# The last down-projection groups by output chunk, the next norm's sums under them, and the second block's output projection as three fp32r products

## The reference: what is computed

```
# first block
h = concatenate([meta, x])
for l in range(2):
    hn = rmsnorm(h, norm1_g[l])
    ...
    h = h + concatenate([attn_out, conv_out]) @ w_out[l]
    hn = rmsnorm(h, norm2_g[l])
    gate, up = split(hn @ w_gate_up[l])
    h = h + (silu(gate) * up) @ w_down[l]        # 2816 -> 1024
h = rmsnorm(h, final_g)                          # the second block's x
# second block
h = rms(x, g_mix) * (1 + sc1) + sh1
proj = h @ w_in
...
merged = sigmoid(gate_a) * (y_a @ w_up_gdn) + sigmoid(gate_b) * (y_b @ w_up_dil)
x = x + gt1 * (merged @ w_out)                   # 1024 -> 1024
h2 = rms(x, g_ffn) * (1 + sc2) + sh2
x = x + gt2 * moe_ffn(h2)
```

## Time and profile before

| what | value |
|---|---|
| median of 3 runs | 1787.42 us (1782.62, 1787.43, 1787.42) |
| the profiled execution's own time | 1784.96 us |
| its span, first to last instruction | 1783.1 us |
| TensorE matmuls busy | 1709.4 us (96%) |
| DVE busy | 910.5 us (51%) |
| ACT busy | 682.7 us (38%) |
| mean granted TensorE clock | 0.983 of 2.4 GHz |
| HBM read | 401.39 MB |

### The profile page before, as it was taken

The page is one execution under the profiler, slowest core; times in us unless marked ns, Lnnn a source line. Parts: engine busy times, 40 slices in busy tenths (PEclk is TensorE's granted clock), DMA queues, the critical chain, the costliest instruction groups (busy, mean ns, idle before and its releaser), DMA issues.

```text
span 1783.1 us, 28470 instructions
## 1 busy us (share of the span) xinstructions
PE 1709.4 (96%) x11058; PEld 1335.9 (75%) x11058; DVE 910.5 (51%) x1612; ACT 682.7 (38%) x1242; POOL 55.8 (3%) x48
## 2 busy tenths in 40 slices
PE   7998999989989999999999999899999999999997
PEld 5777999987779999977889899898545454545453
DVE  4957666438757665367765778844211212121212
ACT  2136444321264443254654377722122222222222
POOL 0001000000010000003220000000000000000000
PEclk9999999999999999998999999998999999999999
DMA  6534454545434555532422344355699999999993
GB/s 272 199 142 144 164 175 179 189 142 195 183 142 146 186 188 189 189 116 95 138 70 78 112 142 142 122 194 231 241 410 422 421 421 422 421 423 421 422 422 151
DMA packets 63956, 404.04 MB, mean 227 GB/s; under 512 B 13056, under 2 KB 14592, under 8 KB 15232
## 3 DMA queue, kind: packets, MB, share of 16 engines
q1 hardware_dynamic: 63440, 401.34, 58.5%
q10 hardware_dynamic: 432, 1.51, 0.2%
HBM read 401.39 MB, written 1.44 MB: 226 GB/s over the span
## 4 chain that ended last, share of the span: by engine, by line
PE 84%; DVE 10%; ACT 4%; issue 1%; DMA 0%; SPq 0%; DVEq 0%; ACTq 0%
PE ps L841 24%; PE ps L1415 20%; PE ps L970 10%; PE ps L643 6%; PE ps L1388 4%; PE ps L1405 4%; DVE big L2210 2%; DVE inv L2442 2%; PE ps L1331 2%; PE ps L1303 1%; PE ps L599 1%; DVE wlo L2620 1%; PE ps L1356 1%; PE ps L1314 1%; PE ps L690 1%
## 5 line engine op out<-in xcount | busy, mean ns | idle before, releaser
L2273 DVE TENSOR_TENSOR wlo<-ring,whi 128x2048 fp32r<-128x2048 f32 x76 | 174.2, 2292 | 111.5 <-ACT whi L1612 111.2
L841 PE MATMUL ps<-hg_hi,wlo 128*128 128x272 f32 (+1 forms) x672 | 191.4, 285 | 0.0
L841 PE MATMUL ps<-hg_hi,whi 128*128 128x272 f32 (+1 forms) x672 | 191.0, 284 | 0.0
L841 PE MATMUL ps<-hn_lo,whi 128*128 128x272 f32 (+1 forms) x672 | 190.8, 284 | 0.0
L1415 PE MATMUL ps<-big 128*64 128x512 f32 x816 | 181.8, 594 | 0.7 <-ACT big L2106 0.7
L1415 PE MATMUL ps<-ring,big 128*64 128x512 f32 x816 | 181.7, 594 | 0.0
L1612 ACT ACTIVATE whi<-ring 128x2048 fp32r<-128x2048 f32 x76 | 144.8, 1905 | 75.3 <-PE ps L841 75.0
L643 PE MATMUL ps<-hn,ring 128*128 128x272 f32 x640 | 160.6, 408 | 8.9 <-DVE hn L2181 5.6
L643 PEld LDWEIGHTS ps<-hn,ring 128*128 128x128 f32 x640 | 123.8, 197 | 41.7 <-issue 16.5
L1415 PEld LDWEIGHTS ps<-big 128*64 128x64 f32 x816 | 57.5, 137 | 107.0 <-issue 106.6
L1415 PEld LDWEIGHTS ps<-ring,big 128*64 128x64 f32 x816 | 57.1, 137 | 107.2 <-issue 106.8
(11 more groups left out here) (447 smaller groups left out, 3481.6 us busy)
## 6 DMA issues: line engine op xcount, KB each, us to landing
ring<-in_stream SPq DMA_DIRECT2D x277, 1024.0 KB, 5.1
big<-in_stream SPq DMA_DIRECT2D x102, 1024.0 KB, 12.9
h<-in_xT SPq DMA_DIRECT2D x1, 1088.0 KB, 5.0
out_xT<-h SPq DMA_DIRECT2D x1, 1024.0 KB, 4.7
big<-in_consts ACTq DMA_DIRECT2D x1, 896.0 KB, 4.9
cst<-in_consts SPq DMA_DIRECT2D x1, 576.0 KB, 6.0
big<-in_consts ACTq DMA_DIRECT2D x1, 326.5 KB, 3.4
from_blocks<-big SPq DMA_DIRECT2D x1, 256.0 KB, 2.0
```

Of the source, the lines that this page charges most:

```text
L841: m = mm(out, a[:, at_:at_ + P], b[:, kept], start=first and i == 0, stop=last and i == 2)
L2273: v.tensor_tensor(wlo[j][:, :], ring[:, j, :], whi[d % 3][:, :], ALU.subtract).then_inc(wlo_ready, 1)
```

## The change

Down projection: half 1 runs its first four groups as before. Then the sums of chunks 0 to 3 of the next norm are issued (plain for layer 1's first norm, weighted at the end of the first block), and the last two groups run with the output chunk as the outer loop, so that 18 products finish one chunk; a semaphore tells DVE of each of the first three. DVE adds them one by one, ACT squares four chunks in one instruction and then one by one. The sums of chunks 4 to 7 stand behind the last product. At the end of the first block the plain sums follow the weighted ones as before.

Output projection: its four slots (now named O0 to O3) and the merged activations are split into high and low parts, as in the slots before, and TensorE does three fp32r products for each f32 one. In O0 the last two input chunks of both output chunks come last. Bank 5 takes O0's second output chunk. DVE's and ACT's new instructions are put between the old ones by hand.

```diff
@@ memory
-    [("yb_hi", BIG0 + 1152, 4, T), ("yb_lo", BIG0 + 2176, 4, T), ("yo_hi", BIG0 + 3200, GH, T), ("yo_lo", BIG0 + 11392, GH, T),
+    [("yb_hi", BIG0 + 1152, 4, T), ("yb_lo", BIG0 + 2176, 4, T), ("yo_hi", BIG0 + 3200, GH, T),
+     ("mg_hi", BIG0 + 5248, GH, T), ("yo_lo", BIG0 + 11392, GH, T),
...
+     ("mg_lo", BIG0 + 19584, GH, T), ("wb0", BIG0 + 27776, SLOT)]]
@@ TensorE
+            def first_sums(l, chunks):
+                cols = of_use(l - 1)
+                for c in chunks:
+                    W(pe, "sq_ready", max(c - 2, 1), l)
+                    m = mm(ps[:, 7, cols], ones, sq[:, c, cols], start=c == 0, stop=c == DC - 1)
+                return m
...
+            def weighted_sum(chunks):
+                for c in chunks:
+                    W(pe, "sq_ready", max(c - 2, 1), DEPTH)
+                    m = mm(ps[:, 7, 0:T], fin_w[:, c:c + 1].to_broadcast([P, P]), sq[:, c, META:L], start=c == 0, stop=c == DC - 1)
+                return m
...
-                norm_sums(l, 0)
+                if l == 0:
+                    first_sums(l, range(4))
+                first_sums(l, range(4, DC)).then_inc(norm_sum, 1)
...
                 for half in range(2):
-                    for g in range(6):
+                    for g in range(6 - 2 * half):
                         w = both_parts(d0 + 6 * half + g)
...
+                if l + 1 < DEPTH:
+                    first_sums(l + 1, range(4))
+                else:
+                    weighted_sum(range(4))
+                w4 = both_parts(d0 + 10)
+                for n in range(4):
+                    m = down(1, 4, w4, n)
+                    if n == 0:
+                        w5 = both_parts(d0 + 11)
+                    if n == 3:
+                        m.then_inc(slot_done, 1)
+                    m = down(1, 5, w5, n)
+                    m.then_inc(slot_done if n == 3 else even_full, 1)
-            both_norms()
+            weighted_sum(range(4, DC)).then_inc(norm_sum, 1)
+            for c in range(DC):
+                m = mm(ps[:, 6, 0:T], ones, sq[:, c, META:L], start=c == 0, stop=c == DC - 1)
+            m.then_inc(norm_sum, 1)
...
-            for j in range(4):
-                w = slot(B2 + OUT2 + j, 0).rearrange("p (k n c) -> p k n c", k=8, n=2)
-                for n in range(2):
-                    for k in range(DC):
-                        if j == 0 and n == 0 and k % 2 == 0:
-                            pe.wait_ge(merged, k // 2 + 1)
-                        m = mm(ps[:, OUT_BANK[j], n * T:(n + 1) * T], w[:, k, n, :], sga[:, k, :], start=k == 0, stop=k == DC - 1)
+            def project_out(name):
+                hi, lo = (w.rearrange("p (k n c) -> p k n c", k=8, n=2) for w in both_of(name))
+                first = name == "O0"
+                for ks in ((range(6), range(6, DC)) if first else (range(DC),)):
+                    for n in range(2):
+                        for k in ks:
+                            if first and n == 0 and k % 2 == 0:
+                                W(pe, "xlo_ready", 4 + k // 2, DEPTH)
+                            for j, (w, y) in enumerate(((hi, mg_hi), (lo, mg_hi), (hi, mg_lo))):
+                                m = mm(ps[:, out_bank(int(name[1]), n), n * T:(n + 1) * T], w[:, k, n, :], y[:, k, :],
+                                       start=k + j == 0, stop=k == DC - 1 and j == 2)
                 m.then_inc(slot_done, 1)
@@ ACT
-            def squares(l, which, need):
+            def squares(l):
                 cols = of_use(l - 1)
-                for g in range(2):
-                    W(act, "h_added", need(g), l)
-                    f(sq[:, 4 * g:4 * g + 4, cols], h[:, 4 * g:4 * g + 4, cols], ACT.Square).then_inc(sq_ready, 1)
+                for i, (a, b) in enumerate(((0, 4), (4, 5), (5, 6), (6, 7), (7, 8))):
+                    if l:
+                        W(act, "h_added", 1 + DC + b, l - 1)
+                    f(sq[:, a:b, cols], h[:, a:b, cols], ACT.Square).then_inc(sq_ready, 1)
...
+            def merged_high(j):
+                act.wait_ge(merged, j + 1)
+                f(mg_hi[:, 2 * j:2 * j + 2, :], sga[:, 2 * j:2 * j + 2, :], ACT.Copy).then_inc(xhi_ready, 1)
             for name in ("UD0", "UD1", "UG2", "UG3"):
                 high_of(name)
+            merged_high(0)
+            merged_high(1)
+            high_of("O0")
+            merged_high(2)
+            high_of("O1")
+            merged_high(3)
+            high_of("O2")
+            high_of("O3")
             token_squares()
@@ DVE
-                dve.wait_ge(slot_done, l * LAYER_SLOTS + LAYER_SLOTS)
                 for n in range(4):
+                    if n < 3:
+                        W(dve, "even_full", IN_SLOTS + OUT_SLOTS + n + 1, l)
+                    else:
+                        dve.wait_ge(slot_done, l * LAYER_SLOTS + LAYER_SLOTS)
                     v.tensor_tensor(h[:, 4 + n, kept], h[:, 4 + n, kept], ps[:, n, kept], ALU.add).then_inc(h_added, 1)
...
+            def merged_low(j):
+                W(dve, "xhi_ready", 4 + j, DEPTH)
+                d = slice(2 * j, 2 * j + 2)
+                v.tensor_tensor(mg_lo[:, d, :], sga[:, d, :], mg_hi[:, d, :], ALU.subtract).then_inc(xlo_ready, 1)
             low_of("UG3")
+            merged_low(0)
+            merged_low(1)
             times_dil(1)
             times_gdn(2)
             merge(2)
+            low_of("O0")
+            merged_low(2)
             times_gdn(3)
             merge(3)
...
+            low_of("O1")
+            merged_low(3)
+            low_of("O2")
+            x_added(0)
+            low_of("O3")
+            for j in range(1, 4):
+                x_added(j)
```

More of the change, by code:

```diff
@@ L81 @@
 SPLIT = ORDER.index("dq0")
+OUTS = ["O0", "O1", "O2", "O3"]
+PLACE = {name: i for i, name in enumerate([*ORDER, *OUTS])}
 EX0 = B2 + OUT2 + 4
@@ L907, in _, with down @@
                 d0 = OUT_SLOTS + GU_SLOTS
+                def down(half, g, w, n):
+                    for k in range(min(4, FC - 4 * g)):
+                        m = product(ps[:, 4 - 4 * half + n, kept], w, (4 * k + n) * P, (hff_hi, hff_lo), 4 * g + k,
+                                    g + k == 0, 4 * g + k == FC - 1)
+                    return m
                 for half in range(2):
-                    for g in range(6):
+                    for g in range(6 - 2 * half):
                         w = both_parts(d0 + 6 * half + g)
@@ L912, in _ @@
                             W(pe, "hff_lo_ready", min(4 * g + 4, FC), l)
[L913 to L916, removed]
+                        for n in range(4):
+                            m = down(half, g, w, n)
                         m.then_inc(slot_done, 1)
[L919 to L927, removed]
-            both_norms()
+                if l + 1 < DEPTH:
[3 more added lines that the diff above has]
+                w4 = both_parts(d0 + 10)
+                for n in range(4):
+                    m = down(1, 4, w4, n)
[9 more added lines that the diff above has]
+            m.then_inc(norm_sum, 1)
             def token_sums():
@@ L1726, in _ @@
                     high_weights(d)
-            squares(DEPTH, 0, lambda g: 1)
+            squares(DEPTH)
             e2 = small[:, 59:60]
@@ L2756, in _, with x_added @@
             merge(1)
+            def x_added(j):
+                dve.wait_ge(slot_done, B2 + OUT2 + j + 1)
+                for n in range(2):
+                    c = 2 * j + n
+                    v.scalar_tensor_tensor(x[:, c, :], ps[:, out_bank(j, n), n * T:(n + 1) * T], mod[:, 16 + c:17 + c], x[:, c, :],
+                                           ALU.mult, ALU.add).then_inc(x_ready, 1)
+            def merged_low(j):
+                W(dve, "xhi_ready", 4 + j, DEPTH)
+                d = slice(2 * j, 2 * j + 2)
+                v.tensor_tensor(mg_lo[:, d, :], sga[:, d, :], mg_hi[:, d, :], ALU.subtract).then_inc(xlo_ready, 1)
             low_of("UG3")
+            merged_low(0)
+            merged_low(1)
             times_dil(1)
```

44 lines of the change are left out of this document (21 added, 23 removed).

## The result

The changed kernel took 1772.44 us (median of five, 1771.60 to 1775.16), the kernel before 1783.93 beside it (1782.62 to 1787.43): a ratio of 0.9935 with a 95% interval of 0.9923 to 0.9947, so faster by about 11.6 us, between 9.5 and 13.7. The forecast was 1772.3 and 13.3 us of gain. Measured again later (e11), it came to 1772.76 and a ratio of 0.9942 (0.9929 to 0.9955).

A forecast was written before the change was run, and what follows sets the result against it. The chain is almost all TensorE matmuls, so time goes where TensorE waits or runs slowly. 4.0 + 5.35 + 3.95 = 13.3 us, against the mean of 1785.6, gives 1772.3 us; range 1766 to 1779.

The forecast's parts named there:

- First seam: From first to second layer of the first block: root starts at 389.55, not 393.56, 4.0 us earlier.
- Rival 2: Square root's table switch at both seams really costs 1.38 us more once exposed: 2.8 us lost, 1775.1; chance 0.04.
- Second seam: Into the second block: root starts at 751.55, not 756.90, 5.35 us earlier.
- the price of a weighted sum at full clock: Sums with the final gain, into the second block: taken as 0.229 us each, like plain ones; other bound 0.42.
- Rival 1: Sums into the second block: broadcast weights are slow by form, 0.42 us at any clock: 1775.4; chance 0.06.
- Output projection: Second block: 192 products in 23.04 us instead of 27.64, 4.60 less, minus a 0.65 us stall: 3.95 us.
- The wait: First slot of the output projection: TensorE stalls about 0.65 us for the last small low part.
- Rival 3: Output projection gives nothing: splits come late through ACT's and DVE's queues, each slot waits a microsecond: 1776.3; chance 0.05.
- The expert stage: Behind the output projection: takes over the gain, stream and TensorE move together; nothing grows or shrinks.
- rivals 4 and 5: Expert stage: stream sets the end, 1785, no measurable change, chance 0.02; or stream slips and TensorE waits, 1796, chance 0.03.
- The stretch behind the first root: Layer 1's input projection starts slowly, 3.65 us for 10 instructions: no change taken, +1.7 and -1.5 kept for the range.

The follow-up runs named there:

- e11: The changed kernel measured again, unaltered, beside the same executions of the kernel before: 1772.76 us, ratio 0.9942.
- e3: Changed kernel with the last two down groups run with the input chunk outside again, moved sums and single squares kept: 1774.11 us, ratio 0.9929.
- e1: Kernel before with only the change's parts on the down projection, norm sums and squares; output projection plain f32: 1776.50 us, ratio 0.9943.
- e4: Changed kernel with all eight chunks' sums behind the last down product, output chunk still the outer loop of the last two groups: 1773.40 us, ratio 0.9924.
- e2: Kernel before with only the change's part on the output projection; down projection and norm sums as before: 1778.71 us, ratio 0.9958.
- e10: Kernel before with five extra f32 products of constants, first layer only, while TensorE waits for its first normalized input: 1784.03 us, ratio 0.9997.
- e9: Kernel before with six extra f32 products of constants between the last down product and the norm sums of each layer: 1777.02 us, ratio 0.9973.
- e5: Changed kernel with DVE making the last small low part of the merged activations before the second output slot's low part: 1771.83 us, ratio 0.9938.
- e6: Changed kernel with extra f32 products of constants, five in the first layer, six in the second, while TensorE waits for normalized input: 1769.45 us, ratio 0.9922.

## Why the prediction was right

**First seam, 4.0 us forecast:** 3.99. Each term of the sum stood: moved sums 1.83, add and square of one chunk 0.45 and 0.43 to DVE's and ACT's handover, table load 1.28, root 2.23 behind the end. ACT was last, as written, not TensorE. No drain around the table load: the Trainium skill ("ScalarE: Activation LUTs", section "What ACT_TABLE_LOAD costs") would have the root 1.38 us later, and in the chain it follows the load with 0.01 us between. Rival 2 is out. What the prediction took as the means was not needed, though: it runs the last groups by output chunk to hide the adds and squares of chunks 4 to 6, and e3 hides them with the input chunk outside, and its root comes as early. And it doesn't name the finer wait of the first square as a source of gain, which it uses and which e1, e3 and e4 have in common.

**Second seam, 5.35 us:** 5.41, measured against the profile from which the forecast took its 9.35. Against the 7.77 and 7.74 us of e2 and e10 it would be 3.8, and the seam before, with its input projection, 5.7 instead of 4.1. The path behind the change was right; that the two numbers meet so closely one by one is the choice of profile, and only their sum of 9.5 stands against all three. The one unknown was the price of a weighted sum at full clock, put at 0.229 from the plain ones; it is 0.216 (1.73 for eight in e1). Rival 1 (slow by form) is out by this and by e9.

**Output projection, 3.95 us:** 3.65, and 23.04 of product time met within 0.02 once the wait was gone (e5). The wait, put at 0.65, costs 0.93 by e5. TensorE's timeline in the changed kernel has it:

```profile
1187.34 0.28 PE L1371 MATMUL ps<-mg_lo,wb 128*128 128x256 f32 x1
1188.30 0.39 PE L1371 MATMUL ps<-mg_hi,wb 128*128 128x256 f32 x1 [0.68 <-DVE mg_lo L2829]
1188.52 0.28 PE L1371 MATMUL ps<-mg_hi,wlo 128*128 128x256 f32 x1
```

The idle time is 0.68, as forecast. But starts are 0.96 apart across it, where 0.12 is usual, and 0.22 behind it: a product's record is 0.28 us long, products overlap, and this overlap is lost once at the wait. That is the term I left out. The place and the order that makes it were right. The estimate worked out from the Trainium skill ("TensorE: Matmul & The Clock Gate", section "Back-to-back issue gap"), 21.0 us by the gap of an isolated matmul, isn't what these products do: e5 has 23.06. Rival 3 had the right queue and too large a price.

**The expert stage** passed the gain on: rivals 4 and 5 didn't happen. Its first products with expert weights (L1415 before) start at 1255.10 instead of 1267.58, 12.48 us earlier, and the span ends 12.5 us earlier. Of the 13.4 us at the end of the output projection 0.9 were lost in the router and shared expert between, where single stages took 0.4 to 0.6 us more.

**The stretch behind the first root** kept its slow start, as assumed: 9.20 against 9.27 us.

What the sum didn't hold is that a low-clock stretch more or less stands at other places too. In the changed kernel's profile there are these, and in the one before the attention of layer 1 looks like this:

```profile
513.00:519.00 6.00, 6.00 (x31) 4.67 (x34) 1.11 (x5) 1.80 (x11) 0.00 (x0) 0.50 0.05 18
1138.00:1144.00 6.00, 5.80 (x27) 5.80 (x28) 4.21 (x3) 4.41 (x4) 0.00 (x0) 0.50 0.14 60
```

```profile
521.00:527.00 6.00, 5.96 (x67) 3.77 (x65) 2.78 (x10) 2.74 (x9) 0.00 (x0) 0.74 0.14 27
```

The whole stretch is at 0.50 after the change and half of it before, and this goes with 1.3 us more in that layer. It was so in six of the seven profiles that have the changed down part and no filled waits (in e1 it is cut in two), and in none of the four with the old one. The order of the last two groups doesn't set it off, since e3 has it with the old order; what does stays open. The forecast's 13.3 against 11.5 us between the medians can't be split into such parts: the spans of the two profiles differ by 12.5, and the rest depends on which executions the medians are. The forecast held, within its range and near its center, also because 1785.6, the mean it started from, lay 1.7 us above the median that was measured beside the changed kernel: two misses of the same size that cancel.

## What to carry to other kernels

A short wait of TensorE has two prices, the wait and the half-speed work after it. At the second seam the second price was 3.0 of 9.35 us in one profile and 1.4 of 7.8 in two others; look at the granted clock behind each idle stretch, in more than one profile, and fill the stretch if it can't be removed. At the end of a reduction, look first at what each helper's wait asks for: here a square waited for additions that it didn't need. Give each finished part its own signal (no run tests these two alone, but all variants without the gap have them), and put the dependent small work behind, not ahead: moving it ahead only reorders the engine that is the bound, and may uncover something that it covered (here ACT's table load). Reordering the products so that parts finish early brought nothing beyond that (e3). When a chain leaves an engine, count its instructions before calling that point the end: 63 of 72 products was not the end. When products are split by two helper engines, give the small part that is needed first the first place in the helper's queue.

## What the runs showed that I had not expected

Idle time can be worth filling with products that nobody reads: the kernel before got 4.8 us faster (2.5 to 7.1) by six of them at each seam (e9), the changed one about 3 us by eleven (e6). But a filled wait can leave the total where it was (e10), and where a gain shows in one profile it may be the place of a low-clock stretch that moved. The kernel's spread of 5 to 6 us from one execution to the next on the same chip goes with the mean granted clock, from 0.984 down to 0.980; which stretches make it isn't settled. A gain below 3 us can't be read off the total of this kernel in eleven executions, but it can be read off its stages, if the stage is cut at the same event in both.
